# A two-block transformer kernel in fp32: mixer branches in three passes, GLA outputs beside the third gates, and one group of low weight parts moved from GpSimd to VectorE

## What is computed

```python
h = rms_norm(x, norm_mix[l])
p_rw, p_s5, p_gla, p_gate = _split(h @ w_in[l], IN_SIZES)
y_rw = rwkv7_mix(p_rw, ...)       # (512, 512)
y_s5 = s5_mix(p_s5, ...)          # (512, 512), ends in y * sigmoid(y @ w_glu + b_glu)
y_gla = gla_mix(p_gla, ...)       # (512, 512)
gates = jax.nn.sigmoid(p_gate).reshape(B, L, N_BRANCH, D_MODEL)
# each y_b @ w_branch[b] is multiplied by its gate, the three are summed,
# and the sum goes through w_out and is added to x
```

## Time and profile before

| | us |
|---|---|
| median of 3 runs | 3390.56 |
| lowest and highest | 3389.36, 3396.81 |
| the profiled execution | 3396.22 |
| its span | 3394.3 |
| mean granted clock of PE | 0.965 of 2.4 GHz |

### The profile page before, as it was taken

How to read it: one execution, slowest core, us unless ns; L and a number is a source line. 1 busy time by engine, 2 the same in 40 slices (tenths; PEclk the granted TensorE clock), 3 DMA queues, 4 the chain that set the end, 5 groups by cost and what they waited for, 6 DMA issues and landing times. The chain is left out here.

```text
span 3394.3 us, 48744 instructions
## 1 busy us (share of the span) xinstructions
PE 3156.8 (93%) x19634; PEld 2458.4 (72%) x19634; DVE 1678.2 (49%) x2586; ACT 1154.4 (34%) x1781; POOL 582.1 (17%) x496
## 2 busy tenths in 40 slices
PE   7988988999998999989787899999989999799998
PEld 5666643576666888867676788888868888678886
DVE  5644489344343666234665333333348878643332
ACT  4211264342123222244675311111244545432222
POOL 0000033000102443150453300000042322100000
PEclk9999999989998999989999899999989999889999
DMA  3476200212321222211000111202121112122222
GB/s 131 177 269 223 88 29 13 92 58 99 124 87 50 79 95 84 103 57 50 26 2 1 50 56 44 94 31 90 34 101 70 57 60 78 50 75 100 99 85 77
DMA packets 33998, 270.56 MB, mean 80 GB/s; under 512 B 3184, under 2 KB 5616, under 8 KB 14576
## 3 DMA queue, kind: packets, MB, share of 16 engines
q1 hardware_dynamic: 33776, 267.46, 21.7%
HBM read 263.25 MB, written 4.19 MB: 79 GB/s over the span
## 5 line engine op out<-in xcount | busy, mean ns | idle before, releaser
L705 PE MATMUL banks<-normed_high,weights_high 128*128 128x512 f32 (+1 forms) x2264 | 852.4, 385 | 59.1 <-DVEq L534 37.4
L705 PE MATMUL banks<-normed_low,weights_high 128*128 128x512 f32 (+1 forms) x2264 | 834.5, 377 | 0.0
L301 DVE TENSOR_TENSOR weights_low<-ring,weights_high 128x1024 fp32r<-128x1024 f32 (+1 forms) x261 | 315.8, 1210 | 716.1 <-ACTq L413 701.6
L411 ACT ACTIVATE weights_high<-ring 128x1024 fp32r<-128x1024 f32 (+1 forms) x309 | 322.5, 1044 | 1009.5 <-PE banks L705 758.9
L705 PEld LDWEIGHTS banks<-normed_high,weights_high 128*128 128x128 f32 x2264 | 436.5, 193 | 173.9 <-issue 44.8
L705 PE MATMUL banks<-normed_high,weights_low 128*128 128x512 f32 (+1 forms) x2264 | 535.1, 375 | 0.0
L705 PEld LDWEIGHTS banks<-normed_low,weights_high 128*128 128x128 f32 x2264 | 437.7, 193 | 81.2 <-issue 4.5
L705 PEld LDWEIGHTS banks<-normed_high,weights_low 128*128 128x128 f32 x2264 | 404.6, 192 | 80.6
L664 POOL TENSOR_TENSOR latent_total<-latent_total,latent_square 128x512 f32<-128x512 f32 x42 | 62.7, 1492 | 1418.5 <-ACTq L643 1418.3
L705 PE MATMUL banks<-ffn_hidden_high,weights_high 128*128 128x512 f32 (+1 forms) x704 | 251.2, 366 | 0.0
L705 PE MATMUL banks<-ffn_hidden_low,weights_high 128*128 128x512 f32 (+1 forms) x704 | 251.2, 366 | 0.0
(11 more groups left out here) (552 smaller groups left out, 4651.7 us busy)
## 6 DMA issues: line engine op xcount, KB each, us to landing
ring<-in_ada SPq DMA_DIRECT2D x48, 1024.0 KB, 6.2
ring<-in_ffn_up SPq DMA_DIRECT2D x22, 2048.0 KB, 7.9
ring<-in_hgrn SPq DMA_DIRECT2D x16, 1536.0 KB, 6.6
ring<-in_ffn_down SPq DMA_DIRECT2D x16, 1408.0 KB, 6.0
ring<-in_gates SPq DMA_DIRECT2D x6, 2048.0 KB, 8.0
ring<-in_wo SPq DMA_DIRECT2D x6, 2048.0 KB, 7.9
ring<-in_ffn_up2a SPq DMA_DIRECT2D x4, 2048.0 KB, 8.0
ring<-in_ffn_up2b SPq DMA_DIRECT2D x4, 2048.0 KB, 7.8
```

What stands on the lines that cost most here:

```text
L301: e.eng.tensor_tensor(out, x, hi.bitcast(F32), ALU.subtract).then_inc(e.sem, e.tick())
L411: e.eng.activation(self.by_k(k.WH), self.source(), ACT.Copy).then_inc(e.sem, e.tick())
L705: mm = pe.matmul(ps[:, 0:y.shape[-1]], w, y, start=(kk == 0 and n == 0), stop=(kk == kt - 1 and n == len(every) - 1))
```

## The change

1. `branch0` to `branch2` are parted like the other sections and done in three passes. The class `MixerParts` makes the high and low parts of the mixer's output: ScalarE copies each tile, DVE subtracts. Their memory lies over columns of RWKV and GLA that are no longer read. In `rwkv_out` the product with G is made in four tiles, so that the parts can follow one by one.
2. The order of sections becomes glu, w_gla, branch1, gates2, branch2. glu now makes two pieces of w_gla ahead. The parts of the S5 output are made beside w_gla's last tile.
3. `gla_outputs` is no block of its own any more: its steps hang beside the tiles of gates2, with one exponential over all four heads in place of four.
4. In branch2 ScalarE makes the high part of the merged sum (DVE did), DVE the low part one tile later; the low parts of branch2's weights are made by GpSimd, but for the first.
5. In the S5 loop the low parts of gates1 are made by DVE, after even steps from the second on, behind `turned` and behind the output where there is one.

```diff
-LOW_BY_GPSIMD = ("ffn_up", "gates1")
+LOW_BY_GPSIMD = ("ffn_up", "branch2")
...
+class MixerParts:
...
+    def high(self, e, t):
+        e.eng.activation(self.hi[:, t, :], self.Y[:, t, :], ACT.Copy).then_inc(self.rounded.sem, 1)
+
+    def low(self, e, t):
+        e.eng.wait_ge(self.rounded.sem, self.rounded.at(t + 1))
+        low_part(e, self.lo[:, t, :], self.Y[:, t, :], self.hi[:, t, :])
+        e.eng.wait_ge(e.sem, e.now())
+        e.eng.sem_inc(self.parted.sem, 1)
...
+    def mixer_ready(pe, part, kk):
+        pe.wait_ge(parts.parted.sem, parts.parted.at(kk + 1))
...
+    linear(k, f"branch{b}", [parts.operand], merge, kt=MT, tiles=8, per=(1, 2, 2)[b], ahead=1, arrive=mixer_ready,
+           begin=dict(vector=gates_kept), aside=aside if b == 2 else None, low_on="gpsimd" if b == 2 else "vector",
+           more=dict(mixer_rounded=MT, mixer_parted=MT))
...
                 g.sem_inc(angles.sem, 1)
-                if i % 2 == 0:
-                    own[i // 2].low(e)
...
                 v.sem_inc(turned.sem, 1)
                 if i and i % 4 == 0:
                     output(i // 4 - 1)
+                if i and i % 2 == 0:
+                    own[i // 2].low(e)
...
+        merge_branch(k, 1, s5_parts, M, G, T1)
+        gates(k, 2, G, gla_outputs(k, KT, W, R, EE, KS[:].rearrange("p a t n -> p (a t) n"), PG, Y, parts), None)
+        merge_branch(k, 2, parts, M, G, T1)
...
+    def by_tensor(pe, n):
+        if n == 0:
+            pe.wait_ge(turned.sem, 1)
+            pe.wait_ge(masked.sem, 1)
             for c in range(NCK - 1):
...
+        if n == 2:
+            pe.wait_ge(states.sem, NCK - 1)
             for h in range(4):
-                pe.wait_ge(squared.sem, squared.at(h + 1))
-                pe.matmul(k.PS[4 + h], k.const("ones"), SQ[:, h, :]).then_inc(summed.sem, 1)
...
+                for c in range(NCK):
+                    mm = pe.matmul(k.PS[4 + h][:, c * C:c * C + C], W[:, c, h // 2, h % 2, :], R[:, h // 2, h % 2, c * C:c * C + C])
+                mm.then_inc(outs.sem, 1)
+        if n == 4:
+            pe.wait_ge(squared.sem, 4)
+            pe.wait_ge(scaled.sem, 1)
+            for h in range(4):
+                mm = pe.matmul(k.PS[4 + h], k.const("ones"), SQ[:, h, :])
+            mm.then_inc(summed.sem, 1)
```

More of the change, by code:

```diff
@@ L983, in col, with gates, gate, __init__ @@
     return k.V[:, VCOL[name] + t:VCOL[name] + t + 1]
[L986 to L1002, removed]
+def gates(k, b, G, aside, more):
+    def gate(e, t, part, ps, at_):
+        e.eng.activation(at(G, t), ps[:], ACT.Sigmoid).then_inc(e.sem, e.tick())
+        e.eng.wait_ge(e.sem, e.now())
+    linear(k, f"gates{b}", [k.H.operand(LAT)], gate, on="scalar", aside=aside, more=more, ahead=1)
+class MixerParts:
+    def __init__(self, k, name, Y, offset):
+        self.Y, size = Y, 4 * MT * L
+        self.hi, self.lo = (k.nc.alloc_sbuf_tensor_at(f"{name}_{x}", [P, MT, L], F32R, offset=offset + n * size)
+                            for n, x in enumerate(("high", "low")))
+        self.rounded, self.parted = k.count("mixer_rounded"), k.count("mixer_parted")
+    def operand(self, kk):
+        return self.hi[:, kk, :], self.lo[:, kk, :]
+    def high(self, e, t):
[3 more added lines that the diff above has]
+        low_part(e, self.lo[:, t, :], self.Y[:, t, :], self.hi[:, t, :])
+        e.eng.wait_ge(e.sem, e.now())
+        e.eng.sem_inc(self.parted.sem, 1)
+def merge_branch(k, b, parts, M, G, T1):
+    kept, taken = k.emptied["scalar"], k.count("s5_gates_taken")
+    merged, rounded, parted = k.count("merges_summed"), k.count("merges_rounded"), k.count("merges_parted")
     def merge(e, t, part, ps, at_):
@@ L1046, in rwkv @@
         k.begin_row()
-        branch(k, 0, Y, M, aside=rwkv_out(k, PR, G, KK, LD, Y))
+        gate = k.sb("rw_gate", [P, DT, L], s)
+        gates(k, 0, gate, rwkv_out(k, PR, G, KK, LD, Y, parts), dict(mix_finished=MT))
+        merge_branch(k, 0, parts, M, gate, None)
 def ada_load(k, sp, n):
@@ L1549, in by_vector @@
             v.wait_ge(e.sem, e.now())
-            v.tensor_tensor(Y[:], Y[:], G[:], ALU.mult).then_inc(e.sem, e.tick())
-            v.wait_ge(e.sem, e.now())
-            v.sem_inc(finished.sem, 1)
+            for t in range(MT):
+                v.tensor_tensor(Y[:, t, :], Y[:, t, :], G[:, t, :], ALU.mult).then_inc(finished.sem, 1)
+        if n == 7:
+            for t in range(MT):
+                parts.low(e, t)
     def by_scalar(e, n):
@@ L1563, in by_scalar @@
             a.sem_inc(rooted.sem, 1)
+        if n == 7:
+            for t in range(MT):
+                a.wait_ge(finished.sem, t + 1)
+                parts.high(e, t)
     return dict(scalar=by_scalar, tensor=by_tensor, vector=by_vector)
@@ L1980, in by_scalar @@
                 a.wait_ge(made.sem, made.at(4))
+                a.wait_ge(s5_gated.sem, s5_gated.at(0))
+                for t in range(MT):
+                    s5_parts.high(e, t)
                 for t in range(2):
@@ L2030, in by_vector @@
                 v.wait_ge(made.sem, made.at(3))
+                for t in range(MT):
+                    s5_parts.low(e, t)
                 for b in range(2):
@@ L2147, in gla_outputs @@
-        ends.update(gla_updates_made=NCK // 2, gla_states_ready=NCK - 1, gla_outputs_made=4, gla_squares_ready=4,
-                    gla_squares_summed=4, gla_roots_ready=4)
+                a.wait_ge(finished.sem, h + 1)
+                parts.high(e, h)
+    return dict(scalar=by_scalar, tensor=by_tensor, vector=by_vector)
 def cross_attention(k):
```

131 lines of the change are left out of this document (67 added, 64 removed), and 4 rows, old and new, of the table SECTIONS.

## The result

The changed kernel takes 3363.25 us (median of 4 runs, 3361.26 to 3365.33), against 3390.93 before (4 runs): a ratio of 0.9915, interval 0.9898 to 0.9932. The prediction was 3362, with a range of 3350 to 3375. The profiled execution took 3364.90 us, its span 3363.1.

A forecast was written before the change was run, and what follows sets the result against it. The prediction took TensorE, busy 93% of the span, to bound the kernel, with DVE setting the S5 loop's pace. Terms -2.5 + 1.6 - 27.7 = -28.6 us against the median 3390.56 gave 3362 us, range 3350 to 3375.

The forecast's parts named there:

- glu to w_out: From glu's end to w_out: 180.3 us in place of 208.0, -27.7 with w_out's +1.0 included, -28.7 without it.
- Branch 0: In branch 0: eight tiles in three passes save 5.1 us, a later start costs 2.6, net -2.5.
- S5 loop: In the S5 loop: low parts on DVE cost 13.7 us in place of 12.1 us of waits, so +1.6.
- the seven terms: S5 loop's seven low parts on DVE: four cost 1.37 us each, three behind an output (steps 4, 8, 12) 2.75.
- The rival of GpSimd first in near ties: S5 loop: GpSimd starts ahead of DVE in three near ties, 6.8 us more, 3369 us; chance 0.14.
- The rival that the GLA work doesn't pack: gates2: GLA groups keep 19.37 us instead of 14.5, +4.9, and branch2 ends late by +4: 3370 us; chance 0.13.
- the slower one: Branches: the two weight buffers don't overlap; at 4.9 us a tile 50.6 us more, 3412 us; chance 0.03.
- w_out's start: w_out's first tile waits for branch2's last merged tile: +1.0 us, between 0 and +4.
- At most 3.5 held: branch2: DVE needs 2.4 us a tile alone, at most 3.5 when held by GpSimd's low parts; PE needs 2.79.

The follow-up runs named there:

- the mid-step one: The changed kernel with the S5 loop's low parts moved to mid-step, behind the second add and ahead of the scans: 3358.4 us, a single execution.
- the kernel with two groups: The changed kernel with the 28 GLA state steps in two groups, 16 and 12, behind gates2's first and second tiles: 3359.1 us, a single execution.

## Why the prediction was right

The terms came out stage by stage, and the large one, from glu to w_out, by the mechanism that was named. That the time came within 1.3 us of the forecast is partly luck: two executions drift by more than that in the same code, and small misses cancelled.

**Branch 0** (-2.5, measured -2.39). The start costs what the parts take: PE waits 0.99 us, then gets parts 0.84 apart, and finishes the first tile 4.9 us after gates0 (391.05); the others are 2.80 apart. Two small misses cancel here. Before, the eight tiles took 414.07 - 387.01 = 27.06 us from first matmul to the next section's first, 3.38 each and not 3.43, so the passes gave 4.7 us and not 5.1; and the start cost 2.3 and not 2.6.

**S5 loop** (+1.6, measured +1.99). Each of the seven terms is in the trace. DVE's low part behind step 2, the gap ahead of step 4, and the low part behind step 4; then GpSimd's angles behind steps 2 and 4:

```profile
465.27 1.23 DVE L301 TENSOR_TENSOR weights_low<-ring,weights_high 128x1024 fp32r<-128x1024 f32 x1
...
475.99 0.69 DVE L1910 TENSOR_TENSOR s_forced<-s_sin_cos,banks 128x512 f32<-128x512 f32 x1 [0.57 <-DVE s_im_parts L1926]
...
485.73 2.59 DVE L301 TENSOR_TENSOR weights_low<-ring,weights_high 128x1024 fp32r<-128x1024 f32 x1
```
```profile
465.33 3.38 POOL L1811 TENSOR_TENSOR s_angles<-s_angles,s_turns 128x1024 f32<-128x1024 f32 x1 [6.53 <-DVEq L1928]
...
484.89 2.35 POOL L1811 TENSOR_TENSOR s_angles<-s_angles,s_turns 128x1024 f32<-128x1024 f32 x1 [6.91 <-DVEq L1928]
```

With 0.06 us of lead DVE had its 1.23, GpSimd lasted 3.38; behind the output GpSimd had started and DVE lasted 2.59. 4 x 1.37 + 3 x 2.75 = 13.7 came out to the hundredth; the 0.4 beyond it is the one gap of 0.57 instead of 0.22 at 475.99, which the kernel with the low part ahead of the output has too and the mid-step one hasn't. Its cause wasn't found. The rival of GpSimd first in near ties fell at 9 of 9 such places in two kernels (3 and 6). DVE's row started 0.06 to 0.07 us earlier at each. The closest pair in the changed kernel's trace is in branch2: DVE's add at 775.20 lasted 0.69 us, GpSimd's low part at 775.22 lasted 1.82 instead of 1.29. GpSimd was first in none of these pairs, so no run shows a near tie that it won. The Trainium skill, SBUF — State Buffer, section "SBUF: two separate sides", gives this rule, first to start has the pair, and asks two SBUF inputs of DVE's side; the trace agrees, 1.49 us of an add becoming 0.69 with one operand in PSUM.

**glu to w_out** (-28.7, measured -29.02). w_gla 74.2 for 74.4; branch1 22.4 for 22.3; gates2 60.0 for 60.3; branch2 with its 0.45 of wait 23.0 for 22.3. These give 28.4. Another 0.55 comes from the forecast's starting point. It took 616.86, the modelled end of glu's row, as glu's end; in the changed kernel the next matmul starts 13.44 us after glu's first, which would be 616.31 before. So the idle stretch that went was 3.8 us long and not 3.21. PE and DVE in gates2:

```profile
717.10 3.27 PE L2143 MATMUL banks<-gla_state_and_v,gla_k_tok 64*64 64x128 f32 x56
...
730.98 2.13 PE L705 MATMUL banks<-normed_high,weights_low 128*128 128x512 f32 x8 [1.10 <-DVEq L433]
732.95 7.25 PE L2150 MATMUL banks<-gla_q_and_scores,gla_state_and_v 128*128 128x64 f32 x64
```
```profile
718.23 11.26 DVE L2168 SCALAR_TENSOR_TENSOR gla_state_and_v<-gla_state_and_v,gla_end,banks 64x128 f32<-64x128 f32 x28 [3.69 <-PE banks L2143]
729.64 2.60 DVE L301 TENSOR_TENSOR weights_low<-ring,weights_high 128x1024 fp32r<-128x1024 f32 x2
```

PE was busy for 58.90 of gates2's 60.00 us. The wait of 1.10 behind the state steps was forecast at 1.2, and the kernel with two groups takes it away. The rival that the GLA work doesn't pack fell, and the slower one too: no branch tile waited for its weights.

**w_out's start** (+1.0, measured +1.70, and 0.45 in branch2): the term that was most mis-sized, within its bounds of 0 to +4. "At most 3.5 held" was worked out, but its consequence wasn't: DVE's tile lasted 3.29 against PE's 2.80, so half a microsecond of lag a tile over five tiles stood at w_out's door. DVE, GpSimd and PE:

```profile
781.18 1.48 DVE L1022 TENSOR_TENSOR residual<-residual,gated 128x512 f32<-128x512 f32 x1
```
```profile
780.82 1.29 POOL L301 TENSOR_TENSOR weights_low<-ring,weights_high 128x512 fp32r<-128x512 f32 x1 [1.06 <-ACTq L413]
```
```profile
799.96 0.50 PE L705 MATMUL banks<-normed_high,weights_high 128*128 128x512 f32 x1 [2.48 <-DVEq L1040]
801.37 2.02 PE L705 MATMUL banks<-normed_high,weights_low 128*128 128x512 f32 x8
```

The kernel with the product in PSUM brings DVE's tile to 2.80, and this wait falls to 0.80 us. The +1.70 is also the lucky one of two outcomes: with the clock falling behind the wait, as in five of nine executions, it would have been 2.9 to 3.3.

**What the parts are worth.** Undone one by one, the passes give 12 us, the overlap 24, the order 6.6 to 9.5, and the move in the S5 loop costs 2. That is more than the whole 27.8, mostly because the group that replaced the overlap is a worse one than the block before: against that block the overlap gives 14.6. A part undone shows that it matters, and its size only against what stands in its place.

## What to carry to other kernels

Work with long waits between small steps belongs beside the passes of a stage that needs nothing of it: it saves the waits and the lower clock behind them. Before moving an operation from GpSimd to VectorE, look where it meets what GpSimd still does: the same seven subtractions cost 14.1, 10.0 or 9.7 us by their place in the step alone. Where an engine falls behind by a fraction of a tile, multiply by the tiles and look at the next stage's first wait; four banks between hide the lag, they don't remove it.

## What was not expected of the hardware

A DVE add with one operand in PSUM wasn't held by GpSimd and didn't hold it (0.69 and 1.29 us side by side), and writing the product to its PSUM bank took 0.70 us against 0.69 to SBUF. A held DVE instruction ends its own length less some 0.14 us behind GpSimd's row: 1.08 us for 1.23 (488.32 behind 487.24), 0.55 for 0.69 (779.81 behind 779.26). Behind the same wait of 2.4 to 2.5 us in w_out PE's granted clock stayed at 1.00 in four executions and fell in five, to a mean of 0.72 or 0.73 over the next 6 us. Why step 4 of the S5 loop starts 0.36 us late is open.
